# Result stores of a mixture-of-experts loop moved from GpSimd's queue to the sync engine's

## What is computed

```python
def expert_block(args):
    toks, e = args
    xb = x_pad[toks]
    hb = jax.nn.silu(xb @ w1[e]) * (xb @ w3[e])
    return hb @ w2[e]
```

## Time and profile before

| | |
|---|---|
| median of three runs | 2992.24 us (2990.52 to 2995.51) |
| profiled execution | 2991.91 us |
| its span | 2990.2 us |
| PE busy | 2739.4 us (92%) |
| DVE busy | 1347.6 us (45%) |
| ACT busy | 963.5 us (32%) |
| POOL busy | 471.7 us (16%) |

### The profile page before, as it was taken

How to read it: one execution, slowest core, us unless ns; L and a number is a source line. 1 busy time by engine, 2 the same in 40 slices (tenths; PEclk the granted TensorE clock), 3 DMA queues, 4 the chain that set the end, 5 groups by cost and what they waited for, 6 DMA issues and landing times. The chain is left out here.

```text
span 2990.2 us, 45603 instructions
## 1 busy us (share of the span) xinstructions
PE 2739.4 (92%) x15137; PEld 1363.8 (46%) x15137; DVE 1347.6 (45%) x2726; ACT 963.5 (32%) x1858; POOL 471.7 (16%) x669
## 2 busy tenths in 40 slices
PE   7999999986899898899999999399999998999978
PEld 3444444432444444444444555255555554455533
DVE  2231414132778687778786777212212221122218
ACT  2222222121777677677771221110001010010004
POOL 0101010101011111121110222211111111111123
PEclk8999999997999999999999999699999999999989
DMA  8020201018586767676664433586896479968737
GB/s 316 14 84 14 74 25 56 14 56 310 160 275 203 265 200 246 205 249 204 230 217 153 148 131 117 204 273 218 288 302 216 149 235 354 351 218 271 241 100 315
DMA packets 275921, 575.74 MB, mean 193 GB/s; under 512 B 59270, under 2 KB 75719, under 8 KB 271740
## 3 DMA queue, kind: packets, MB, share of 16 engines
q1 hardware_dynamic: 192936, 427.99, 41.4%
q0 software_dynamic: 82480, 145.43, 15.3%
q10 hardware_dynamic: 324, 0.10, 0.0%
HBM read 460.86 MB, written 112.29 MB: 192 GB/s over the span
## 5 line engine op out<-in xcount | busy, mean ns | idle before, releaser
L1930 PE MATMUL h<-w,xT 128*64 128x256 f32 x5120 | 589.0, 383 | 22.2 <-DMA w<-in_w 18.1
L1930 PEld LDWEIGHTS h<-w,xT 128*64 128x64 f32 x5120 | 362.7, 138 | 244.6 <-issue 75.2
L1220 DVE TENSOR_TENSOR_SCAN left<-leave,left 128x512 f32<-128x512 f32 (+3 forms) x320 | 358.7, 1121 | 159.0 <-ACT leave L1102 157.9
L418 PE MATMUL bank<-xnT,w_in 128*128 128x512 f32 x768 | 330.3, 592 | 0.0
L1943 PE MATMUL yb<-w,hT 128*64 128x512 f32 x1280 | 309.4, 604 | 0.0
L1911 ACT ACTIVATE sg<-h 128x128 f32<-128x128 f32 x160 | 44.3, 277 | 692.1 <-PE h L1930 692.1
L1023 POOL DMA_DIRECT2D w_out<-in_cache_v x256 | 137.4, 537 | 689.2 <-issue 687.6
L1589 PE MATMUL pb<-w_out,featT 128*128 128x512 f32 x512 | 227.7, 597 | 2.2 <-DVE t L1654 2.2
L418 PEld LDWEIGHTS bank<-xnT,w_in 128*128 128x128 f32 x768 | 145.6, 190 | 181.8 <-issue 180.6
L1976 DVE TENSOR_TENSOR sg<-sg,h 128x128 f32<-128x128 f32 x160 | 46.1, 288 | 388.0 <-ACT sg L1911 388.0
L418 PE MATMUL bank<-w_in,xnT 128*128 128x512 f32 x512 | 220.4, 592 | 0.0
(11 more groups left out here) (372 smaller groups left out, 2873.9 us busy)
## 6 DMA issues: line engine op xcount, KB each, us to landing
w<-in_w SPq DMA_DIRECT2D x96, 2048.0 KB, 23.8
w_out<-in_cache_v POOLq DMA_DIRECT2D x256, 256.0 KB, 5.0
w_out<-in_cache_k SPq DMA_DIRECT2D x256, 256.0 KB, 3.9
ys_d<-zeros SPq DMA_DIRECT2D x32, 816.0 KB
slab<-in_w_ada SPq DMA_DIRECT2D x24, 1024.0 KB, 17.9
ys_d<-y POOLq DMA_DIRECT2D x83, 256.0 KB, 9.8
x_in<-xs_d POOLq DMA_DIRECT2D x162, 128.0 KB, 6.3
w_in<-in_w_in SPq DMA_DIRECT2D x5, 2048.0 KB, 20.3
```

The costliest lines, as they stand in the source:

```text
L418: mm = pe.matmul(ps[:, :], w, m, start=(i == 0), stop=(i == len(parts) - 1))
L1220: dve.tensor_tensor_scan(left[n % 4][:, 0:cols][:, ::-1], leave[n % 4][:, 0:cols][:, ::-1], leave[n % 4][:, 0:cols][:, ::-1], left[n % 4][ ...
L1930: mm = pe.matmul(h[half][q * G:q * G + G, 0:2 * P], xT[:, c % (XW // P), c // (XW // P) * G:c // (XW // P) * G + G], w13[i][:, c, :, cols] ...
```

## The change

SP walks through the blocks too. Its loop over an expert's blocks issues the stores, one per block; after the loop it waits until PE has finished the expert's last block and issues the weights for three experts later. The store of zeros, the two last stores and the final wait move to SP as well. POOL keeps only the loads. Sizes, waits and the numbering of the stores stay as they are.

```diff
             @block.sync
             def _(sp):
-                done = sp.alloc_register("blocks_done")
-                sp.reg_mov(done, 0)
-                sp.wait_ge(s["in"], 32)
-                for e in range(NE):
+                x1_rows = io["x1_d"][0:SEQ, :].rearrange("(t p) n -> p t n", p=P)
+
+                def weights(e):
                     i = e % SLOTS
-                    if e >= SLOTS:
-                        sp.reg_add(done, done, blocks_of(sp, e - SLOTS))
-                        hold(sp, s["y"], sp.snap(done, min_val=1, max_val=MAX_BLOCKS), s["sp"])
                     if e > 0:
                         for at, name in enumerate(("w1", "w3")):
                             sp.dma_start(w13[i][:, :, at, :], ...).then_inc(s_w13[i], 16)
                     sp.dma_start(w2[i][:, :, :], ...).then_inc(s_w2[i], 16)
...
+                def store(n):
+
+                    hold(sp, s["ye"], n + 1, s["sp"])
+                    hold(sp, s["st"], 16 * n + 16, s["sp"])
+                    sp.dma_start(strips(io["ys_d"], n * G + G), y[:, ds(n & 1, 1), :].rearrange("p a n -> p (a n)")).then_inc(s["st"], 16)
+
+                sp.wait_ge(s["in"], 32)
+                for e in range(SLOTS):
+                    weights(e)
+                sp.nop().then_inc(s["ye"], 2)
+                sp.wait_ge(s["go"], 1)
+                sp.dma_start(strips(io["ys_d"], 0), y[:, 0, :]).then_inc(s["st"], 16)
+                count = sp.alloc_register("blocks_stored")
+                sp.reg_mov(count, 0)
+                for e in range(NE):
+                    with sp.Fori(0, blocks_of(sp, e)):
+                        store(sp.snap(count, min_val=0, max_val=MAX_BLOCKS))
+                        sp.reg_add(count, count, 1)
+                    if e < NE - 1:
+                        hold(sp, s["y"], sp.snap(count, min_val=1, max_val=MAX_BLOCKS), s["sp"])
+                    if e + SLOTS < NE:
+                        weights(e + SLOTS)
+                    elif e == NE - 3:
+                        sp.dma_start(keep["x1_a"], x1_rows[:, 0:8, :]).then_inc(sems["x1_a"], 16)
+                        sp.dma_start(keep["x1_b"], x1_rows[:, 8:12, :]).then_inc(sems["x1_b"], 16)
+                    elif e == NE - 2:
+                        sp.dma_start(keep["x1_c"], x1_rows[:, 12:16, :]).then_inc(sems["x1_c"], 16)
+                        sp.dma_start(keep["x1_s"], io["x1_d"][SEQ:, :]).then_inc(sems["x1_s"], 16)
+                n = sp.snap(count, min_val=NE, max_val=MAX_BLOCKS)
+                store(n)
+                store(n + 1)
+                hold(sp, s["st"], 16 * n + 48, s["sp"])
...
             @block.gpsimd
             def _(pool):
-                pool.nop().then_inc(s["ye"], 2)
                 pool.nop().then_inc(s["xT"], 1)
-                pool.wait_ge(s["go"], 1)
-                pool.dma_start(strips(io["ys_d"], 0), y[:, 0, :]).then_inc(s["st"], 16)
...
-                def store(n):
...
                 def body(n, e, b, offs):
                     load(n, pool.snap(e * CAP + offs + b * G))
-                    store(n)
 
                 n = experts(pool, body, before)
                 load(n, 0)
-                store(n)
-                store(n + 1)
-                hold(pool, s["st"], 16 * n + 48, s["sp"])
                 hold(pool, s["in"], 32 * n + 32, s["sp"])
```

More of the change, by code:

```diff
@@ L1879, in load @@
                         pool.dma_start(x_in[64 * half:64 * half + 64, :], strips(io[f"xs_d{half}"], row)).then_inc(s["in"], 16)
-                def store(n):
-                    hold(pool, s["ye"], n + 1, s["sp"])
-                    hold(pool, s["st"], 16 * n + 16, s["sp"])
-                    pool.dma_start(strips(io["ys_d"], n * G + G), y[:, ds(n & 1, 1), :].rearrange("p a n -> p (a n)")).then_inc(s["st"], 16)
                 def before(e):
```

## The result

The changed kernel takes 3343.76 us (median of four runs, 3339.87 to 3348.19); the kernel before, run beside it, 2993.61 us. The ratio is 1.117, with a 95% interval of 1.1153 to 1.1186: 350 us slower. I had forecast 3388 us, 396 us slower.

The account below looks back on a forecast made before the run. PE was taken to bound the experts stage, busy 943 of 983 us. Rounds 380, first round 33 and residual loads 13, less 30 gained, make +396 us on 2991.9: 3388 us, range 3150 to 3540 us (8 in 10).

Parts of the forecast that it names:

- store landed, into the round: Store behind a round of weights on SP's queue: weights 18.0, store 6.0, fixed latency 2.5, landing 26.5 us into the round.
- PE's stall: PE waits for the copy into `y` behind the late store: 26.5 + 1.6 - 17.3 = 10.8 us per round.
- clock per stall: PE runs at half clock around a stall, costing 1.6 or 3.0 us; 2.3 us taken.
- 29 rounds: All 29 rounds of weights in the experts stage cost the same 13.1 us: 380 us.
- first round: Start of the stage: zeros and store 0 stand behind seven weight DMAs; stall 31 us, with clock 33 us.
- behind 6 MB of `x1`: Residual loads after expert 29: 6 MB go ahead of a store, one more stall of 13 us.
- waits that go from the kernel before: POOL's loads no longer stand behind stores: late `x_in` and weight waits and their clock go, at most 31, taken 30 us.
- start and end of the stage: At the end, two stores and a wait move between engines with nothing ahead of them: no cost.
- Does a store pass the weights?: On SP's queue it does not: 128 KB land in 3.8 us alone, 11.4 with 2 MB issued just ahead.
- No second stall: The store after the late one finds an empty queue, lands some 8.5 us later; next copy due after about 10 us.
- Same order, shorter wait: Rival, chance 0.24: store spread over 16 engines or moving beside the weights; 6.9 us per round, +200 us, 3192 us.
- Faster: Rival, chance 0.08: a store on SP's queue lands 11.5 us into the round, copy never late; 2962 us.

Follow-up runs that it names:

- experiment 7: The changed kernel, with only the first quarter of `w2` loaded for experts 3 to 31, 4.5 MB ahead of the store instead of 6 MB: 3214.1 us, ratio 1.075.
- experiments 2: The changed kernel, with rounds of weights for experts 3 to 31 cut to 1 MB instead of 6 MB: 2987.9 us in one run, beside 2990.0 for the kernel before.
- experiment 8: The kernel before the change, with each of GpSimd's stores as two DMAs of 64 partitions, which 16 DMA engines can share: 2958.7 us, ratio 0.9899.
- experiment 5: Against the kernel before: stores issued by ScalarE on its own queue, each as two DMAs of 64 partitions, which 16 engines can share: 2951.3 us, ratio 0.9873.
- experiments 3: The changed kernel, with each store on SP as two DMAs of 64 partitions, which 16 DMA engines can share: 3219.1 us, ratio 1.0767.
- experiment 4: Against the kernel before: stores issued by ScalarE on its own queue, SP keeping only the weights and GpSimd only the loads: 3148.1 us, ratio 1.0527.

## Why the prediction was right

**The mechanism and its sum.** It was the store behind each round of weights on SP's queue. By terms:

| term | predicted | measured |
|---|---|---|
| store landed, into the round | 26.5 us | 25.5 us at DVE's copy |
| PE's stall | 10.8 us | 10.0 us (30 stalls) |
| clock per stall | 2.3 us | 2.4 us (12.4 - 10.0) |
| 29 rounds | 380 us | 29 x 12.4 = 360 us |
| first round | 33 us | 30.6 us |
| behind 6 MB of `x1` | 13 us | 11.7 us |
| waits that go from the kernel before | -30 us | -38.6 us |
| start and end of the stage | 0 | -8 us |

I forecast +396 us; the two profiled spans differ by 356. The 40 us between are 20 from the rounds, 9 from the gain, 8 from start and end and 4 from the two single stalls. The medians differ by 350.

**The size of the landing.** The sum was right within 1 us, and the DMA rows say in which part. In the round shown, `w2` landed 20.7 us after the round began (2147.8 against 2127.18), where 18.0 + 2.5 = 20.5 stood for the weights and the fixed part; the store was there 4.9 us later, where I took 6.0. I had let it move at the 21.9 GB/s per engine of the weights' stretch; alone, its two engines moved 51 GB/s, 25.5 each. The rate by which the landing follows the bytes, 374 GB/s by experiment 7, is a little above the 350 that I took.

**Does a store pass the weights?** The prediction leaned on 11.4 us against 3.8 for 128 KB, and that compared a load behind 2 MB with a store that had nothing ahead. It was a thin support for the right answer; the DMA view of the changed kernel and experiments 2 and 7 are what shows it.

**"No second stall."** It held: every block that isn't the first behind a round takes 11.6 us. Experts of one block cost about as much per round as the others, as I had argued.

**The clock.** The bounds of 1.6 and 3.0 us from two stalls held the value. In the stall shown the clock is 0.50 until 5.6 us after PE resumed, and half of that is 2.8 us; the block took 24.7 - 11.6 - 10.4 = 2.7 us beyond its stall.

**The gain** was under-counted. I had counted waits that the profile names for `x_in` and weights; the blocks of the kernel before lost 38.6 us against 11.6 us each, and the changed kernel lost nothing outside its stalls. Not all of it was the price of POOL's stores. With these on 16 engines (experiment 8) or on ScalarE (experiment 5) PE still waits 9 to 10 us for weights among the experts of one block, and in experiment 8 two blocks there take 14 us too many. The changed kernel and experiments 3 and 7, the three with a stall behind every round, don't have these waits: the stalls give the weights that time. It isn't that the stores left GpSimd, as the prediction had it.

**The rivals.** "Same order, shorter wait" fell with the store's start after the weights and with the 5 us on two engines. "Faster" needed a store to pass the weights. The Trainium skill's advice that simple stores go on the sync engine, which is generally faster (DMA: Bandwidth & Descriptors, "Issuing engine by pattern"), would have made it 2962 us; the runs say that the path matters less than what stands ahead on it. With 16 engines on both, ScalarE's queue (experiment 5) and GpSimd's (experiment 8) can't be told apart.

**What the prediction's step missed.** I priced the two engines only as 6 us behind the weights. That the queues of SP and ScalarE give all stores to the same two, so that their load can set the pace, was no part of it; in the changed kernel PE's stalls seem to leave these engines enough time, since the sum holds without that term, and experiment 4 laid it open.

## What to carry to other kernels

Before a transfer is moved to another issuing engine, ask what stands ahead of it there, in bytes and not in instructions, and when its consumer needs the landing: 6 MB ahead are 20.7 us to the landing of the last of them here, whatever the issuing engine's idle time says. Then look at how many DMA engines a transfer uses: a share of 0.11 while it moves alone means two, and giving it 16 was worth 31 us in the kernel before and 197 us on ScalarE's queue. A chain in which each transfer waits for the landing of the one before has its own pace, to be summed for a whole period and not for one transfer.

## What the runs showed of the hardware

- A store with an outer dimension of 2 runs on two DMA engines on either path (share 0.11 to 0.14 of 16). Issued by ScalarE, it shares its two with the last of SP's weights (2.2 engines for both together), and `w2` lands after 27.4 us (median); spread over 16 engines, after 21.1. Issued by GpSimd, the same store costs less: 24.8 us, and 21.6 when spread. That the engines are the same ones each time is inferred from the load, not read off.
- A small load behind a store on GpSimd's queue takes 6.3 us to land, and 3.3 us when the store is spread over 16 engines, with the same weights beside it.
- 6.29 MB of weights ahead on SP's queue are landed 20.7 us after the first is issued, in the round shown, with GpSimd's loads beside them. What 1.57 MB fewer save is 4.2 us, which is 374 GB/s.
